# RWKV core in an fp32 model kernel: both norm sums as 512-column products, roots taken in place in PSUM

## The chip, the cores and the metric

The kernel runs on one core of one Trainium2 chip. The metric is the device time of one execution in microseconds (us); lower is better. Nothing runs on the other seven cores.

## The reference, cut to what matters

The model is a stack of blocks over 1024 tokens and 1024 channels, batch 1, all in fp32: a Hawk layer, an RWKV-7 layer, each with a SwiGLU and a gated embedding step, then a second kind of block. The change is in the RWKV-7 layer alone, in its core, which works on 16 heads of 64 channels:

```python
kk = heads(k * k_k)
kk = kk / jnp.maximum(jnp.sqrt(jnp.sum(kk * kk, axis=-1, keepdims=True)), 1e-12)
...
y = rwkv7_scan(rh, heads(decay), kh, vh, -kk, kk * ah)
mean = jnp.mean(y, axis=-1, keepdims=True)
var = jnp.mean(jnp.square(y - mean), axis=-1, keepdims=True)
yn = ((y - mean) * lax.rsqrt(var + RW_GN_EPS)).reshape(B, T, D)
yn = yn * ln_w.astype(f32) + ln_b.astype(f32)
bonus = jnp.sum(rh * kh * r_k.astype(f32), axis=-1, keepdims=True) * vh
out = (yn + bonus.reshape(B, T, D)).astype(x.dtype) * g
```

So there are two norms over the 64 channels of a head, for each token: the length of the key `kk`, and the deviation of the output `y`. Both want a sum of squares and a reciprocal root.

## The kernel before, in words

Data lie with channels on the 128 partitions and the 1024 tokens along the rows. `rw_core` takes 128 channels at a time, which is one pair of heads, so its loop over `m` has 8 passes (KD = 8), written out without a hardware loop. Tokens are worked in 16 chunks of 64 (NC = 16), two to a tile of 128 (NT = 8). In a pass:

- **grams and transposes** (L1317, L1337, L1339, L1327): products of keys and receivers within each chunk, and four transposed tensors for each tile.
- **the doubling chain**: a triangular 64x64 block of each chunk and head is inverted in five levels, each for two heads h = 0, 1. A level is `corrections` on TensorE (L1359), `keep_correction` on ScalarE (L1539 and L1541, PSUM to SBUF), `inverses` on TensorE (L1368) and `grow` on VectorE (L1718 and L1720). GpSimd masks the off-diagonal part (L1247). The last level has smaller products (L1375, L1382), and `whole` on VectorE (L1725) puts the result together.
- **solutions** (L1391), then **outputs** (L1414 and L1400), which wait for copies on ScalarE (L1588).
- **the prior pass's recurrence**: 15 small steps (`step` L1271/L1273 on TensorE, `state` L1678/L1679 on VectorE) for pair m-1 are threaded through the pass of pair m up to the second level. So the group norm of pair m-1 is taken in pass m, and the key norm of pair m+1 too.

Both norms go the same way. `token_sums` (L1279) makes 8 products whose weights are the 128x128 squares of one tile of tokens and whose moving operand is two columns of a constant (`head_mean`, 1/64 within a head); that leaves one number for each token and head, 128x16 in PSUM. `moment` on VectorE (L1623, L1626) copies the numbers to a small tile, scales them and adds or bounds; `inverse_roots` on ScalarE takes Ln and Exp of 128x32 numbers for both norms at once (L1526, L1527), each with its own table load. `spread` on TensorE (L1287) then makes 16 products with 128 columns for each norm, which bring the rates back to all 128 rows and 1024 tokens in two PSUM banks. `unit_key` (L1631) and `group_norm` (L1685) on VectorE multiply by them. A third sum, `bonus_sum`, already uses `head_sum`: two products of 512 columns with `head_mean` as data for all rows (L1263). In fp32 each of these products is two records in the trace, so `head_sum` shows as x4, `token_sums` as x16, `spread` as x32.

The order on each engine is written by hand, one queue for each engine, and semaphores join them. Around the change TensorE's queue is: `inverses` of level 1, `corrections` of level 2, `variance(m-1)`, `key_sum(m+1)`, `inverses` 2, `corrections` 3, `key_spread(m+1)`, `inverses` 3, `last_corrections`, `deviation_spread(m-1)`, `last_inverses`, `solutions`, `bonus_sum(m+1)`, `outputs`. On VectorE `group_norm(m-1)` and `key_rate(m+1)` stand ahead of `whole`. PSUM banks 2 and 3 (SUM_BANK) hold the key rates, banks 4 and 5 (STEP_BANK) the steps and later the deviation rates.

## Time and profile before

| | us |
|---|---|
| median of 3 runs | 4240.67 (4226.02 to 4241.39) |
| the profiled execution, its own time | 4249.0 |
| its span | 4247.1 |
| TensorE busy in the span | 3794.7 (89%) |
| VectorE, ScalarE, GpSimd busy | 1644.6, 981.1, 1322.8 |
| pace of the core's passes (start of L1414 in two passes) | 75.2, 75.0, 75.2, 71.7, 75.2, 71.4, and 61.0 for the last |

The profile is one execution. Engines are PE (TensorE matmul), PEld (its weight loads), DVE (VectorE), ACT (ScalarE), POOL (GpSimd). A timeline row gives start, length, engine, line, operation, output<-inputs, count, and in brackets how long the engine was idle before it and who released it. PEclk is the granted clock of TensorE: 1.00 is 2.4 GHz, 0.50 is 1.2 GHz. The core is only some 620 us of the span, from about 1863 to 2485 us.

### The profile page before, as it was taken

To read this page: it belongs to the slowest core of one execution; us is meant where nothing else is said; L and a number is where in the kernel's file an instruction comes from. 1 tells how busy PE (TensorE), PEld (TensorE's weight loads), DVE (VectorE), ACT (ScalarE), POOL (GpSimd) and SP (SyncE) were. 2 spreads that over 40 slices of the span, in tenths; PEclk is the share of its full clock that TensorE was granted. 3 is DMA by queue.
4 is the path that set the end of the run, shared out by engine and by line. 5 is a ranking of instruction groups with operands and counts; after the bars stand their busy time and mean duration, and the time that the engine had idled before them with its cause. 6 is when DMAs were issued, how large, how long until landed. Compare 5 with 4: busy or idle time off the path is not lost. (4 is left out here: it accounts for less than half of the span.)

```text
span 4247.1 us, 62128 instructions
## 1 busy us (share of the span) xinstructions
PE 3794.7 (89%) x26524; PEld 3058.4 (72%) x26524; DVE 1644.6 (39%) x1835; ACT 981.1 (23%) x1222; POOL 1322.8 (31%) x989
## 2 busy tenths in 40 slices
PE   5997999999998679978898979999999989977888
PEld 4775788888876467768787857888888777763567
DVE  5554331221344621134645533312213454157542
ACT  3552110000021632223343312100000230141221
POOL 1442233333332122222333312333333323274242
PEclk9998999999999789987878889999999999978899
DMA  2111111111110222220211021111111112100211
GB/s 80 44 41 38 35 49 45 48 46 46 43 56 29 109 81 85 82 99 27 72 37 67 18 80 40 49 45 48 46 45 44 56 38 79 50 7 1 75 45 64
DMA packets 59363, 221.80 MB, mean 52 GB/s; under 512 B 6576, under 2 KB 6832, under 8 KB 58672
## 3 DMA queue, kind: packets, MB, share of 16 engines
q1 hardware_dynamic: 49968, 185.57, 12.8%
q10 hardware_dynamic: 9216, 33.56, 2.0%
q8 instruction: 146, 2.39, 0.2%
q14 instruction: 33, 0.27, 0.0%
HBM read 181.36 MB, written 37.75 MB: 52 GB/s over the span
## 5 line engine op out<-in xcount | busy, mean ns | idle before, releaser
L141 PE MATMUL ps<-xh,whi 128*128 128x512 f32 x4160 | 1343.3, 405 | 190.3 <-DVE xl L343 48.3
L141 PE MATMUL ps<-xl,whi 128*128 128x512 f32 x4160 | 1328.9, 401 | 0.0
L141 PE MATMUL ps<-xh,wlo 128*128 128x512 f32 x4160 | 1327.9, 401 | 0.0
L141 PEld LDWEIGHTS ps<-xh,whi 128*128 128x128 f32 x4160 | 794.3, 192 | 408.3 <-issue 136.1
L141 PEld LDWEIGHTS ps<-xl,whi 128*128 128x128 f32 x4160 | 797.0, 192 | 194.9
L141 PEld LDWEIGHTS ps<-xh,wlo 128*128 128x128 f32 x4160 | 795.5, 191 | 194.3
L115 POOL TENSOR_TENSOR gap<-ones 128x1 f32<-128x1 f32 x258 | 68.6, 266 | 2352.1 <-PE ps L141 2271.8
L118 POOL TENSOR_TENSOR wlo<-wraw,whi 128x1024 fp32r<-128x1024 f32 (+3 forms) x258 | 642.9, 2492 | 21.5
L116 POOL TENSOR_SCALAR whi<-wraw 128x1024 fp32r<-128x1024 f32 (+3 forms) x258 | 285.5, 1107 | 0.0
L572 DVE TENSOR_TENSOR h<-ps,h 128x1024 f32 x56 | 68.5, 1224 | 423.9 <-PE ps L141 423.9
L644 ACT ACTIVATE sq<-sq 128x1024 f32<-128x1024 f32 x44 | 46.6, 1059 | 775.6 <-DVE sq L658 775.6
L658 DVE TENSOR_TENSOR sq<-ps,sq 128x1024 f32<-128x1024 f32 x44 | 53.9, 1225 | 319.2 <-PE ps L141 319.2
L664 DVE TENSOR_TENSOR sum_of_squares<-ps,sq 128x1024 f32<-128x1024 f32 x44 | 53.9, 1225 | 273.5 <-PE ps L141 273.1
L646 ACT ACTIVATE xh<-sum_of_squares 128x1024 f32 x44 | 46.7, 1062 | 437.5 <-DVE sum_of_squares L664 437.5
L899 DVE SCALAR_TENSOR_TENSOR mix<-rw_xn,rw_rest,mix 128x1024 f32<-128x1024 f32 x48 | 62.3, 1308 | 206.2 <-ACT mix L872 206.2
L1247 POOL TENSOR_TENSOR rw_levels<-rw_levels,rw_masks 128x512 f32<-128x512 f32 x64 | 87.4, 1378 | 171.6 <-PE ps L1359 128.4
L660 DVE TENSOR_TENSOR sq<-sq 128x1024 f32<-128x1024 f32 x44 | 103.2, 2345 | 49.5 <-ACT sq L644 49.5
L666 DVE TENSOR_TENSOR xl<-sum_of_squares,xh 128x1024 f32 x44 | 93.3, 2121 | 58.9 <-ACT xh L646 58.9
L336 DVE TENSOR_TENSOR sum_of_squares<-sum_of_squares,sq 128x1024 f32<-128x1024 f32 x48 | 86.8, 1809 | 62.5 <-ACT sq L325 41.7
L316 ACT ACTIVATE gap<-ones 128x1 f32<-128x1 f32 x56 | 11.4, 203 | 350.9 <-DVE h L572 196.2
L1368 PE MATMUL ps<-rw_inverse 64*64 64x32 f32 x2048 | 85.2, 244 | 3.6 <-ACT rw_inverse L1541 3.6
L1368 PEld LDWEIGHTS ps<-rw_inverse 64*64 64x64 f32 x2048 | 81.1, 166 | 6.3 <-ACT rw_inverse L1541 4.3
(402 smaller groups left out, 3837.3 us busy)
## 6 DMA issues: line engine op xcount, KB each, us to landing
wraw<-w_ffn_in SPq DMA_DIRECT2D x88, 512.0 KB, 3.2
rw_kept<-rw_stage ACTq DMA_DIRECT2D x48, 512.0 KB, 2.6
rw_next<-rw_kept SPq DMA_DIRECT2D x40, 512.0 KB, 5.7
wraw<-w_ffn_out SPq DMA_DIRECT2D x32, 512.0 KB, 3.2
wraw<-w_ple SPq DMA_DIRECT2D x16, 640.0 KB, 3.9
wraw<-w_b_in SPq DMA_DIRECT2D x18, 512.0 KB, 3.2
wraw<-w_hawk_in SPq DMA_DIRECT2D x10, 640.0 KB, 3.8
wraw<-w_ffn_out SPq DMA_DIRECT2D x16, 384.0 KB, 2.9
```

What stands on the lines that cost most here:

```text
L115: nc.gpsimd.tensor_tensor(g.gap[:, 0:1], g.ones[:, 0:1], g.ones[:, 0:1], ALU.mult)
L116: nc.gpsimd.tensor_scalar(g.whi[:, s, 0:w], g.wraw[:, s, 0:w], 1.0, 0.0, ALU.mult, ALU.add).then_inc(g.w_hi.sem, 1)
L118: nc.gpsimd.tensor_tensor(g.wlo[:, s, 0:w], g.wraw[:, s, 0:w], g.whi[:, s, 0:w].bitcast(F32), ALU.subtract).then_inc(g.w_split.sem, 1)
L141: last = nc.tensor.matmul(acc[:, hf, :], w[:, s, c:c + P], x[:, kt, hf * HALF:(hf + 1) * HALF], start=start and kt == 0 and n == 0, stop=s ...
L336: nc.vector.tensor_tensor(g.sumsq[:], g.sumsq[:], sq[:, s, :], ALU.add).then_inc(g.sq_used.sem, 1)
L572: nc.vector.tensor_tensor(ht, flat(banks(g, acc + 2 * s)), ht, ALU.add).then_inc(g.acc_free.sem, 1)
L658: nc.vector.tensor_tensor(sg, flat(banks(g, 0)), tmp.rstd, ALU.mult).then_inc(g.gate_scaled.sem, 1)
L660: nc.vector.tensor_tensor(sg, sg, tmp.rstd, ALU.mult).then_inc(g.up_scale.sem, 1)
L666: nc.vector.tensor_tensor(flat(hl[:, bass.ds(m, 1), :]), hid[:], flat(hh[:, bass.ds(m, 1), :]).bitcast(F32), ALU.subtract).then_inc(g.acc_ ...
L899: nc.vector.scalar_tensor_tensor(mix[:, kt % 3, :], xn[:, kt, 1:1 + T], rest[:, 8 * n + kt:8 * n + kt + 1], mix[:, kt % 3, :], ALU.mult, A ...
L1247: nc.gpsimd.tensor_tensor(halved(Nm[:, h]), twice(Nc[:, h]), mask_wide(f"off{b}"), ALU.mult).then_inc(g.off_ready.sem, 1)
L1368: last = nc.tensor.matmul(block_bank(D_BANK + h)[rows, j, :], X[rows, h, j, :], D[rows, h, j, :], start=True, stop=True)
```

## The change

Both sums become `head_sum`: 2 products of 512 columns whose result stands in all 128 rows at once, in the banks where the rates are wanted. ScalarE takes Ln and Exp over 128x1024 in place in those PSUM banks. `token_sums`, `spread` and `moment` go, with the small tiles. The lower bound of the key norm becomes a bias of 1e-37 in the Ln and a minimum of 1e12 in `unit_key`. Lines on each engine move as below.

```diff
@@ TensorE
                 def variance(m):
                     pe.wait_ge(g.dev_ready.sem, g.dev_ready.base + m + 1)
-                    token_sums(dev, DEV_AT, g.var_done)
+                    head_sum(dev, STEP_BANK, g.var_done)

                 def key_sum(m):
                     pe.wait_ge(g.kksq_ready.sem, g.kksq_ready.base + m + 1)
-                    token_sums(t1, KEY_AT, g.kksum_done)
-                def key_spread(m):
-                    pe.wait_ge(g.rates_ready.sem, g.rates_ready.base + m + 1)
-                    spread(SUM_BANK, KEY_AT, g.kkinv_ready)
-                def deviation_spread(m):
-                    pe.wait_ge(g.rates_ready.sem, g.rates_ready.base + m + 3)
-                    spread(STEP_BANK, DEV_AT, g.gn_ready)
+                    head_sum(t1, SUM_BANK, g.kksum_done)
...
                     for h in (0, 1):
                         inverses(m, 1, h)
+                    if following:
+                        pe.wait_ge(g.w_ready.sem, g.w_ready.base + 2 * m + 2)
+                        key_sum(m + 1)
                     for h in (0, 1):
                         corrections(m, 2, h)
                     if prior:
                         variance(m - 1)
-                    if following:
-                        key_sum(m + 1)
...
-                        key_spread(m + 1)
...
-                        deviation_spread(m - 1)
@@ ScalarE
-                def inverse_roots(n):
-                    act.wait_ge(g.moments_ready.sem, g.moments_ready.base + n + 1)
-                    ca.link(act, nc.scalar.activation(moments, moments, ACT.Ln))
-                    nc.scalar.activation(rates, moments, ACT.Exp, scale=-0.5).then_inc(g.rates_ready.sem, 1)
+                key_rates, deviation_rates = (g.ps[:, b:b + 2, :] for b in (SUM_BANK, STEP_BANK))
+                def log_key(m):
+                    act.wait_ge(g.kksum_done.sem, g.kksum_done.base + m + 1)
+                    nc.scalar.activation(key_rates, key_rates, ACT.Ln, scale=float(HD), bias=tiny).then_inc(g.kklog_ready.sem, 1)
+                def inverse_key(m):
+                    act.wait_ge(g.kklog_ready.sem, g.kklog_ready.base + m + 1)
+                    nc.scalar.activation(key_rates, key_rates, ACT.Exp, scale=-0.5).then_inc(g.kkinv_ready.sem, 1)
+                def log_variance(m):
+                    act.wait_ge(g.var_done.sem, g.var_done.base + m + 1)
+                    nc.scalar.activation(deviation_rates, deviation_rates, ACT.Ln, bias=norm_eps).then_inc(g.log_ready.sem, 1)
+                def inverse_deviation(m):
+                    act.wait_ge(g.log_ready.sem, g.log_ready.base + m + 1)
+                    nc.scalar.activation(deviation_rates, deviation_rates, ACT.Exp, scale=-0.5).then_inc(g.gn_ready.sem, 1)
...
                     keep_correction(m, 1, 1)
+                    if following:
+                        growth(m + 1)
                     if prior:
                         squares(m - 1)
                     keep_correction(m, 2, 0)
                     if following:
-                        growth(m + 1)
+                        log_key(m + 1)
                     keep_correction(m, 2, 1)
-                    inverse_roots(m + 1)
+                    if prior:
+                        log_variance(m - 1)
                     keep_correction(m, 3, 0)
                     if following:
-                        blend(m + 1)
+                        inverse_key(m + 1)
                     keep_correction(m, 3, 1)
                     if following:
+                        blend(m + 1)
+                    keep_correction(m, LAST, 0)
+                    if following:
                         decay_until(m + 1)
-                    keep_correction(m, LAST, 0)
                     keep_correction(m, LAST, 1)
+                    if prior:
+                        inverse_deviation(m - 1)
@@ VectorE
-                    nc.vector.tensor_tensor(halves(kk), halves(kk), g.ps[:, SUM_BANK:SUM_BANK + 2, :], ALU.mult).then_inc(g.unit_ready.sem, 1)
+                    nc.vector.scalar_tensor_tensor(halves(kk), g.ps[:, SUM_BANK:SUM_BANK + 2, :], 1e12, halves(kk), ALU.min, ALU.mult).then_inc(g.unit_ready.sem, 1)
...
-                    moment(m + 1 if following else None, m - 1 if prior else None)
                     grow(m, 2, 0)
                     grow(m, 2, 1)
                     grow(m, 3, 0)
                     if following:
                         unit_key(m + 1)
                     grow(m, 3, 1)
-                    if prior:
-                        group_norm(m - 1)
                     if following:
                         key_rate(m + 1)
                     whole(m, 0)
                     whole(m, 1)
+                    if prior:
+                        group_norm(m - 1)
```

The first and the last pass have the same edits for what they hold of it: `key_sum(0)`, `log_key(0)` and `inverse_key(0)` ahead of the loop, `variance(7)`, `log_variance(7)` and `inverse_deviation(7)` behind it.

**TensorE, from the second level to `last_inverses`**, in a pass with a prior and a following pair. Before (L1368 is `inverses`, L1359 `corrections`, L1279 the two sums, L1287 the two spreads, L1375 and L1382 the last level):

```order
L1359 MATMUL ps<-rw_inverse,rw_levels 64x32 x32
L1279 MATMUL ps<-rw_masks,rw_end 128x2 x8
L1279 MATMUL ps<-rw_masks,rw_next 128x2 x8
L1368 MATMUL ps<-rw_inverse 64x32 x32
L1359 MATMUL ps<-rw_inverse,rw_levels 64x32 x32
L1287 MATMUL ps<-ident,wraw 64x128 x16
L1368 MATMUL ps<-rw_inverse 64x32 x32
L1375 MATMUL ps<-rw_inverse,rw_levels 32x32 x32
L1287 MATMUL ps<-ident,wraw 64x128 x16
L1382 MATMUL ps<-rw_inverse 32x32 x32
L1391 MATMUL ps<-rw_tok,rw_inverse 64x128 x32
```

And now (L1344 `inverses`, L1335 `corrections`, L1261 both sums, L1351 and L1358 the last level, L1367 `solutions`):

```order
L1344 MATMUL ps<-rw_inverse 64x32 x32
L1261 MATMUL ps<-rw_next,rw_masks 128x512 x2
L1335 MATMUL ps<-rw_inverse,rw_levels 64x32 x32
L1261 MATMUL ps<-rw_end,rw_masks 128x512 x2
L1344 MATMUL ps<-rw_inverse 64x32 x32
L1335 MATMUL ps<-rw_inverse,rw_levels 64x32 x32
L1344 MATMUL ps<-rw_inverse 64x32 x32
L1351 MATMUL ps<-rw_inverse,rw_levels 32x32 x32
L1358 MATMUL ps<-rw_inverse 32x32 x32
L1367 MATMUL ps<-rw_tok,rw_inverse 64x128 x32
```

The key sum now stands ahead of the second `corrections`, both spreads are gone, and nothing but the chain itself stands between the variance sum and `solutions`.

**ScalarE, from the second level to the copies behind `solutions`.** Before (L1539 and L1541 are `keep_correction`, L1513 `growth`, L1518 `blend`, L1522 `decay_until`):

```order
L1513 ACTIVATE rw_next<-rw_next 128x1024
L1539 ACTIVATE rw_inverse<-ps,rw_masks 128x8x32 [waits x_done]
L1541 ACTIVATE rw_inverse<-ps,rw_masks 128x8x32
L1526 ACT_TABLE_LOAD
L1526 ACTIVATE wraw<-wraw 128x32 [waits moments_ready]
L1527 ACT_TABLE_LOAD
L1527 ACTIVATE wraw<-wraw 128x32 [waits act_chain]
L1539 ACTIVATE rw_inverse<-ps,rw_masks 128x8x32 [waits x_done]
L1541 ACTIVATE rw_inverse<-ps,rw_masks 128x8x32
L1518 ACTIVATE rw_next<-rw_next,rw_small,vectors 128x1024 [waits cum_ready,risen]
```

And now (L1522 and L1524 `keep_correction`, L1498 and L1502 the key's Ln and Exp, L1506 the Ln of the variance):

```order
L1498 ACT_TABLE_LOAD
L1498 ACTIVATE ps<-ps,wraw 128x1024 [waits kksum_done]
L1522 ACTIVATE rw_inverse<-ps,rw_masks 128x8x32 [waits x_done]
L1524 ACTIVATE rw_inverse<-ps,rw_masks 128x8x32
L1506 ACTIVATE ps<-ps,wraw 128x1024 [waits var_done]
L1522 ACTIVATE rw_inverse<-ps,rw_masks 128x8x32 [waits x_done]
L1524 ACTIVATE rw_inverse<-ps,rw_masks 128x8x32
L1502 ACT_TABLE_LOAD
L1502 ACTIVATE ps<-ps 128x1024 [waits kklog_ready]
L1522 ACTIVATE rw_inverse<-ps,rw_masks 128x8x32 [waits x_done]
L1524 ACTIVATE rw_inverse<-ps,rw_masks 128x8x32
L1488 ACTIVATE rw_next<-rw_next,rw_small,vectors 128x1024 [waits cum_ready,risen]
```

Each table load with its activation of 1024 columns now stands between the two halves of a level of the chain; there are two loads to a pass as before.

**VectorE, the end of the chain.** Before (L1685 is `group_norm`, L1636 `key_rate`, L1725 `whole`):

```order
L1720 STREAM_TRANSPOSE rw_inverse<-rw_inverse 128x256 [waits d_ready]
L1685 SCALAR_TENSOR_TENSOR rw_end<-rw_end,vectors,ps 128x1024 [waits gn_ready]
L1636 TENSOR_TENSOR rw_next<-rw_next 128x1024 [waits blend_ready]
L1725 SCALAR_TENSOR_TENSOR rw_inverse<-ps,rw_masks,rw_inverse 128x8x32 [waits blocks_ready,d_done] x2
L1642 SCALAR_TENSOR_TENSOR rw_next<-rw_next,vectors 128x1024 [waits rv_loaded,key_ready]
```

And now (L1668 `group_norm`, L1619 `key_rate`, L1708 `whole`):

```order
L1703 STREAM_TRANSPOSE rw_inverse<-rw_inverse 128x256 [waits d_ready]
L1619 TENSOR_TENSOR rw_next<-rw_next 128x1024 [waits blend_ready]
L1708 SCALAR_TENSOR_TENSOR rw_inverse<-ps,rw_masks,rw_inverse 128x8x32 [waits blocks_ready,d_done] x2
L1668 SCALAR_TENSOR_TENSOR rw_end<-rw_end,vectors,ps 128x1024 [waits gn_ready]
L1625 SCALAR_TENSOR_TENSOR rw_next<-rw_next,vectors 128x1024 [waits rv_loaded,key_ready]
```

`whole`, for which `solutions` waits, no longer stands behind the group norm of the prior pair.

## Rows read from the trace of the kernel before

**Rows 1.** Windows: whole core, then three stretches of pass 4 (length, busy by engine, PEclk)

```profile
1862.60:2485.30 622.70, 532.59 (x12288) 488.53 (x12288) 324.38 (x616) 233.99 (x368) 178.86 (x119) 0.81 0.13 46
2192.00:2205.00 13.00, 12.14 (x401) 11.74 (x396) 9.41 (x25) 8.40 (x14) 5.52 (x4) 1.00 0.02 4
2206.00:2222.50 16.50, 16.50 (x196) 16.36 (x195) 1.99 (x6) 8.17 (x14) 3.75 (x3) 0.50 0.01 2
2233.00:2236.50 3.50, 2.78 (x26) 2.81 (x28) 3.47 (x5) 0.00 (x0) 0.00 (x0) 0.52 0.03 7
```

**Rows 2.** Timeline of TensorE in pass 4, second level to the bonus sum

```profile
2204.17 1.10 PE L1359 MATMUL ps<-rw_inverse,rw_levels 64*64 64x32 f32 x32
2205.43 1.60 PE L1359 MATMUL ps<-rw_inverse,rw_levels 64*64 64x32 f32 x32 [0.17 <-DVE rw_inverse L1720]
2206.96 3.57 PE L1279 MATMUL ps<-rw_masks,rw_end 128*128 128x2 f32 x16
2210.40 3.55 PE L1279 MATMUL ps<-rw_masks,rw_next 128*128 128x2 f32 x16
2213.88 3.63 PE L1368 MATMUL ps<-rw_inverse 64*64 64x32 f32 x64
...
2220.85 2.96 PE L1287 MATMUL ps<-ident,wraw 128*64 128x128 f32 x32
2223.74 2.06 PE L1368 MATMUL ps<-rw_inverse 64*64 64x32 f32 x64
...
2228.41 1.97 PE L1287 MATMUL ps<-ident,wraw 128*64 128x128 f32 x32
...
2233.72 5.08 PE L1391 MATMUL ps<-rw_tok,rw_inverse 64*64 64x128 f32 x64 [2.22 <-issue]
2238.74 1.98 PE L1263 MATMUL ps<-rw_next,rw_masks 128*128 128x512 f32 x4
```

**Rows 3.** Timeline of ScalarE in pass 4

```profile
2205.32 0.47 ACT L1539 ACTIVATE rw_inverse<-ps,rw_masks 128x256 f32<-128x256 f32 x1 [1.21 <-PE ps L1359]
2205.69 0.47 ACT L1541 ACTIVATE rw_inverse<-ps,rw_masks 128x256 f32<-128x256 f32 x1
2206.05 1.05 ACT L1513 ACTIVATE rw_next<-rw_next 128x1024 f32<-128x1024 f32 x1
...
2207.93 1.28 ACT L1526 ACT_TABLE_LOAD   x1
2214.28 0.23 ACT L1526 ACTIVATE wraw<-wraw 128x32 f32<-128x32 f32 x1 [5.07 <-DVE wraw L1626]
2214.52 1.28 ACT L1527 ACT_TABLE_LOAD   x1
2215.82 0.23 ACT L1527 ACTIVATE wraw<-wraw 128x32 f32<-128x32 f32 x1
...
2237.10 1.02 ACT L1588 ACTIVATE rw_levels<-ps 128x1024 f32<-128x1024 f32 x1 [8.10 <-PE ps L1391]
```

**Rows 4.** Timeline of VectorE in pass 4

```profile
2204.38 0.42 DVE L1718 TENSOR_TENSOR rw_inverse<-ps,rw_inverse 128x256 f32<-128x256 f32 x1 [0.70 <-PE ps L1368]
2204.84 0.45 DVE L1720 STREAM_TRANSPOSE rw_inverse<-rw_inverse 128x256 f32<-128x256 f32 x1
2213.99 0.17 DVE L1623 TENSOR_SCALAR wraw<-ps 128x16 f32<-128x16 f32 x1 [8.70 <-PE ps L1279]
...
2230.42 1.28 DVE L1685 SCALAR_TENSOR_TENSOR rw_end<-rw_end,vectors,ps 128x1024 f32<-128x1024 f32 x1 [2.69 <-PE ps L1287]
...
2232.75 0.87 DVE L1725 SCALAR_TENSOR_TENSOR rw_inverse<-ps,rw_masks,rw_inverse 128x256 f32<-128x256 f32 x2
```

**Rows 5.** Timeline: TensorE's `solutions` of passes 0 and 7, the last variance sum

```profile
1936.58 5.17 PE L1391 MATMUL ps<-rw_tok,rw_inverse 64*64 64x128 f32 x64 [0.86 <-DVE rw_inverse L1725]
...
2443.39 3.71 PE L1391 MATMUL ps<-rw_tok,rw_inverse 64*64 64x128 f32 x64 [0.98 <-issue]
...
2473.45 3.57 PE L1279 MATMUL ps<-rw_masks,rw_end 128*128 128x2 f32 x16 [1.42 <-ACT rw_end L1531]
```

More of the change, by code:

```diff
@@ L1128, in rw_core @@
         k_rest, pc = small[:, 0:KD], small[:, KD:KD + NC]
-        moments, rates = (g.wraw[:, 0, KD * P + 2 * HD + n * 4 * NT:KD * P + 2 * HD + (n + 1) * 4 * NT] for n in (0, 1))
-        KEY_AT, DEV_AT = 0, 2 * NT
+        tiny, norm_eps = (g.wraw[:, 0, KD * P + 2 * HD + n:KD * P + 2 * HD + n + 1] for n in (0, 1))
         sw, a, r, kx, v, c, e1, e2, kk, t1 = (nxt[:, n, :] for n in range(10))
@@ L1163, in rw_core @@
         halves = lambda ap: ap.rearrange("p (a b) -> p a b", a=2)
-        sums = g.ps[:, STEP_BANK, 0:P]
         step_bank = lambda cc: g.ps[:, STEP_BANK + cc % 2, 0:2 * CH]
@@ L1274, in step @@
                     last.then_inc(g.st_done.sem, 1)
-                def token_sums(src, at, done):
-                    for j in range(NT):
-                        last = nc.tensor.matmul(sums[:, at + 2 * j:at + 2 * j + 2], src[:, j * P:(j + 1) * P], head_mean[:, 0:P:HD], start=True, stop=True)
-                    last.then_inc(done.sem, 1)
-                def spread(b, at, done):
-                    for j in range(NT):
-                        for h, hd in enumerate(heads):
-                            rate = rates[:, at + 2 * j + h:at + 2 * j + h + 1].broadcast_to([P, HD])
-                            last = nc.tensor.matmul(g.ps[hd, b + j // 4, j % 4 * P:(j % 4 + 1) * P], rate, g.ident[:], start=True, stop=True)
-                    last.then_inc(done.sem, 1)
                 def variance(m):
                     pe.wait_ge(g.dev_ready.sem, g.dev_ready.base + m + 1)
-                    token_sums(dev, DEV_AT, g.var_done)
+                    head_sum(dev, STEP_BANK, g.var_done)
                 def key_sum(m):
                     pe.wait_ge(g.kksq_ready.sem, g.kksq_ready.base + m + 1)
-                    token_sums(t1, KEY_AT, g.kksum_done)
-                def key_spread(m):
-                    pe.wait_ge(g.rates_ready.sem, g.rates_ready.base + m + 1)
-                    spread(SUM_BANK, KEY_AT, g.kkinv_ready)
-                def deviation_spread(m):
-                    pe.wait_ge(g.rates_ready.sem, g.rates_ready.base + m + 3)
-                    spread(STEP_BANK, DEV_AT, g.gn_ready)
+                    head_sum(t1, SUM_BANK, g.kksum_done)
                 def bonus_sum(m):
@@ L1546, in _ @@
                 key_square(0)
-                inverse_roots(0)
+                log_key(0)
+                inverse_key(0)
                 decay(0)
@@ L1595, in _ @@
                 squares(KD - 1)
-                inverse_roots(KD + 1)
+                log_variance(KD - 1)
+                inverse_deviation(KD - 1)
             @block.vector
@@ L1618, in decay_before @@
                         ins.then_inc(g.cum_ready.sem, 1)
-                def moment(key, dev_of):
-                    if key is not None:
-                        dve.wait_ge(g.kksum_done.sem, g.kksum_done.base + key + 1)
-                        ins = nc.vector.tensor_scalar(moments[:, KEY_AT:KEY_AT + 2 * NT], sums[:, KEY_AT:KEY_AT + 2 * NT], float(HD), 1e-24, ALU.mult, ALU.max)
-                    if dev_of is not None:
-                        dve.wait_ge(g.var_done.sem, g.var_done.base + dev_of + 1)
-                        ins = nc.vector.tensor_scalar(moments[:, DEV_AT:DEV_AT + 2 * NT], sums[:, DEV_AT:DEV_AT + 2 * NT], 1.0, GN_EPS, ALU.mult, ALU.add)
-                    ins.then_inc(g.moments_ready.sem, 1)
                 def unit_key(m):
                     dve.wait_ge(g.kkinv_ready.sem, g.kkinv_ready.base + m + 1)
-                    nc.vector.tensor_tensor(halves(kk), halves(kk), g.ps[:, SUM_BANK:SUM_BANK + 2, :], ALU.mult).then_inc(g.unit_ready.sem, 1)
+                    nc.vector.scalar_tensor_tensor(halves(kk), g.ps[:, SUM_BANK:SUM_BANK + 2, :], 1e12, halves(kk), ALU.min, ALU.mult).then_inc(g.unit_ready.sem, 1)
                 def key_rate(m):
@@ L1735, in _ @@
                 decay_before(0, 1)
-                moment(0, None)
                 unit_key(0)
@@ L1829, in _ @@
                     state(KD - 1, cc)
-                moment(None, KD - 1)
                 group_norm(KD - 1)
@@ L1844 @@
                 ("mask_loaded", 16), ("rw_loaded", 48 * KD), ("rv_loaded", 32 * KD), ("gate_loaded", 16 * KD), ("att_stored", 16 * KD),
-                ("rest_ready", 1), ("moments_ready", KD + 2), ("rates_ready", KD + 2)])
+                ("rest_ready", 1)])
 NH = 8
@@ L2828, in make_signals @@
     g.gram_ar = signal("gram_ar")
-    g.moments_ready = signal("moments_ready")
+    g.kklog_ready = signal("kklog_ready")
     g.out_hm = signal("out_hm")
-    g.rates_ready = signal("rates_ready")
+    g.log_ready = signal("log_ready")
     g.rest_ready = signal("rest_ready")
```

10 lines of the change are left out of this document (3 added, 7 removed).

## The prediction

> **What bounds the kernel now.** I read the windows first. The core is 622.7 us of a span of 4247, with a mean granted clock of 0.81 [rows 1]; all that changes is in it. It has 8 passes, and the paces in the table (75.2 to 71.4 us) say that they repeat, so I follow pass 4 by its timelines. The reader is to see three things. First, from 2206.96 to 2233.72 TensorE hardly rests: sums, chain and spreads stand in one queue, and the chain is late because the norms stand in it [rows 2]. Second, this happens at half clock: from 2206 to 2222.5 TensorE is busy 16.50 of 16.50 us at 0.50, that is 1.2 GHz, while the 13 us before it ran at 1.00 [rows 1]; 64 records of `inverses` take 3.63 us there and 2.06 us after the clock has risen [rows 2]. Third, `solutions` start at 2233.72, right behind `whole` (two from 2232.75, done at 2233.62), and `whole` stood behind `group_norm` at 2230.42, which had waited for the second spread [rows 2, 4]. The bracket says "issue", but the end of `whole` fits to 0.1 us. So the time of a pass from the second level to `solutions` is TensorE's queue, then VectorE's behind a spread.
>
> **The change, step by step, in pass 4.** The point of comparison is the start of `solutions`, 2233.72. I walk the new queues from 2204.17, where the second `corrections` began. Prices, all from rows: a half level of 32 records on TensorE 1.0 at high clock (2.06 for two), 1.8 at low (3.63 for two); `head_sum` 1.98, 1.9 to the next start [rows 2]; `keep_correction` 0.84 (two of 0.47, 0.37 apart) [rows 3]; `grow` 0.91 (2204.38 to 2205.29) [rows 4]; a table load 1.28 [rows 3].
>
> The Ln and Exp of 1024 columns in place in PSUM are not in this trace. Nearest are a PSUM to SBUF copy of the same shape, 1.02, and an Exp from SBUF to SBUF, 1.05; the one of 32 columns takes 0.23 [rows 3]. No row writes PSUM from ScalarE, so the ends are 0.85 (the copy less its overlap with a neighbour, some 0.1 to 0.2) and 2.1 (twice the copy). I take 1.05, by the row of the same function.
>
> - *Removed on TensorE:* two sums, 2206.96 to 2213.88, and two spreads, 2220.85 to 2223.74 and 1.9 at 2228.41 [rows 2]: 11.7 us. *Added:* two `head_sum`, 3.8. `moment` (0.17 [rows 4]) goes; `unit_key` stays one pass over PSUM, at most the 1.28 of `group_norm`, which is of its kind [rows 4]; it lies in the wait for level 3 and would cost 0.1 without that cover.
> - *Key sum* at 2204.2, as `key_square` and the w copies are done by then; `corrections` 2 from 2206.1 to 2208.1; variance to 2210.0. `squares` is 1.05 later behind `growth`, ready near 2205.3, so it is covered.
> - *ScalarE, level 2:* keep at 2207.2, done 2208.1; load and Ln (1.28 + 1.05) to 2210.4; the other keep to 2211.3. `inverses` 2 run 2210.0 to 2212.3: only 0.3 is lost. `log_variance` fits behind, to 2212.3. In a queue this is the new wait: behind Ln stands the second keep, and for it the second half of TensorE's level.
> - *Level 3:* `corrections` 2212.3 to 2214.3. Keep to 2214.2; load and Exp to 2216.6; second keep to 2217.4. The second `inverses` cannot start before 2217.5, though TensorE is free at 2215.3: 2.2 us of new idle time.
> - *Last level:* at high clock `inverses` 1.0, `grow` 0.9, last corrections 0.7, keep behind `decay_until`, last inverses 0.6, `whole` 0.5, gives 2222.4. At low clock from about 2214 it gives 2224.0 (`inverses` 1.8, the two small products 1.0 each). I take 2224.0: the stretch from 2210 on has only 32-column products and gaps, as the stretches had before the clock fell.
> - *Behind it:* `group_norm` needs `inverse_deviation`, ready about 2223.4, and is no longer ahead of `whole`. `solutions` are as slow as before (5.08 [rows 2], begun at low clock then too: 0.52 in 2233 to 2236.5 [rows 1]), so their cost does not change. The next thing to be late would be GpSimd's `hats`, behind `group_bias` and `gated`; by the same walk they end within 1 us of when TensorE wants them, so I count nothing.
>
> Gain of a full pass: 2233.7 - 2224.0 = 9.7 us. The six passes 1 to 6 give 58. Pass 0 has only the key norm: the same walk from its second level ends near 1930.8 against 1936.58 [rows 5], 5.8. Pass 7 has only the variance: one spread and one sum at mixed clock less 1.9, and the lower levels in part at high clock, 7 before 2443.39 [rows 5]. Ahead of the loop the key norm ends some 2 us sooner, but `blend`, behind it on ScalarE, is not sooner: 0. At the end the variance of pair 7 is alone: before, 3.57 for the sum [rows 5], 0.2, then 0.23 + 1.28 + 0.23 [rows 3], then a spread; now a sum at low clock (twice 1.9), Ln 1.05, load and Exp 2.33: 2 less. Sum 58 + 5.8 + 7 + 2 = 73. The profiled execution took 4249.0, so it would take 4176; the median is 8.3 lower than that execution, so 4168.
>
> The Trainium skill's page "ScalarE: Activation LUTs", section "What ACT_TABLE_LOAD costs", speaks against this place for the loads: it gives 1.28 us for the load and 1.38 more for a drain with each switch. By it both half levels would wait 1.4 us longer, 2.8 in each of 7 passes, some 19 in all, and the time would be 4187. The trace has a load of 1.28 between an activation that ends at 2214.51 and one that starts at 2215.82 [rows 3]: no drain is seen, so I leave it out of the sum.
>
> **Rivals.**
>
> *B, the clock stays as it is now.* The fall at 2206 comes before the first removed product, amid the chain's 32-column products [rows 1, 2]. If the two sums of 512 columns don't hold it up, everything from 2206 to 2223 runs at 1.2 GHz: `corrections` 2 to 2209.6, variance (3.7) to 2213.1, three half-clock pairs to 2223.5, with 0.7 for Exp, `solutions` at 2228.7; as the clock rose at 2223 before, some 1 us less. Gain 5 to 7 in a pass, 46 in all with 10 for the ends: 4195. For it: the fall did not wait for the 2-column sums. Against: those are 7 us of nearly no columns within the low stretch, and in their place come 3.8 us of dense ones. The Trainium skill's page "TensorE: Matmul & The Clock Gate", section "What's actually happening", says that the gate follows how busy the array has been recently. The trace disagrees if busy means busy time: 16.50 of 16.50 us at half clock. By that rule the new idle gaps would make the clock no better, which is this rival.
>
> *C, the clock stays high through the chain.* `solutions` at 2222.4 and themselves at high clock, 3.71 as in pass 7 [rows 5], against 5.08. Then `hats` bind after about 1 us. Gain 11.5 in a pass, 87 in all: 4154. For it: 13 us of 32-column products with a few wider ones ran at 1.00 [rows 1]. Against: from 2210 on nothing wide is left, and the gaps are larger.
>
> *D, ScalarE is dearer than I think*: an activation in place takes the 2.1 of the upper end, or a load waits as long for other reasons. Two of them hold a half level, so 2.1 in each of 7 passes and as much at the end, some 17 less gain: 4185. For it, that reading and writing PSUM at once is in no row; against it, the 1.02 for reading [rows 3].
>
> *E, slower.* ScalarE becomes the bound. Two activations of 1024 columns stand within the chain, and two more beside it. If one in place in PSUM cost 1.05 + x, a pass would lose 2x at once and up to 4x when ScalarE is full; the gain of 9.7 is gone at x = 2.4 to 4.9. At 4.5 us each (x = 3.45) all four count: 13.8 - 9.7 = 4.1 in a pass, some 30 in all, 4271. For it only that no row writes PSUM from ScalarE; against it, that the copy out of PSUM is no dearer than Exp in SBUF [rows 3].
>
> *F, no difference:* a later wait takes the gain, such as `hats`, or TensorE's fetch gaps at the start of a pass. It would have to be 7 us or more in each pass, and I find only 1.
>
> **How the numbers follow.** Forecast 0.50, B 0.22, C 0.12, D 0.09, F 0.04, E 0.03. The likeliest case alone reaches from 4158 to 4180. The range of 4143 to 4205 takes in B, C and D, with the 15 us over which the three runs lie (4226 to 4241), and leaves out E, F and the outer parts of the others. Over 0.5% (21 us, about what a measurement of this kernel can tell) faster are the forecast, B, C and D with some doubt: 0.91; same 0.05; slower 0.04.
>
> **What would show each step.** In the new profile the stretch from the first `head_sum` of a pass to its `solutions` should be near 20 us (it was 26.8 from the first sum, and 29.5 from the second `corrections`). `head_sum` in the chain should read 1.98 for x4, not 3.7; if 3.7, B. ScalarE's Ln and Exp should read near 1.05; 2 or more means D or E. TensorE should show an idle of about 2 us in level 3, released by `keep_correction`. The low stretch should be under 12 us for a pass, against 16.5. The pass should pace at 64 to 66 us. The prediction is wrong if the pace moves by less than 5 us while the sums read 1.98, for then another engine holds the pass.

## The result, and the profile after

The changed kernel takes 4171.27 us (median of 4 runs, 4165.62 to 4182.99), the kernel before 4240.05 in the same comparison: ratio 0.9849, 95% interval 0.9818 to 0.988. It is faster by 1.5%, 69 us. The prediction said 4168. The profiled execution took 4175.08 with a span of 4173.2, against 4249.0 and 4247.1.

Windows of the changed kernel, as [rows 1]: the core, then pass 4 from the key sum on.

```profile
1860.60:2411.40 550.80, 461.11 (x11584) 393.52 (x11584) 325.20 (x600) 261.54 (x380) 183.94 (x119) 0.85 0.14 51
2172.00:2183.00 11.00, 10.63 (x227) 7.89 (x224) 2.82 (x7) 7.48 (x12) 4.35 (x3) 1.00 0.01 1
2183.00:2196.50 13.50, 11.88 (x240) 11.31 (x238) 9.01 (x12) 7.06 (x10) 3.44 (x2) 0.50 0.01 2
```

The core went from 622.7 us to 550.8, and TensorE's busy time in it from 532.6 to 461.1. The stretch with both sums and level 2 runs at 1.00 now; the clock falls at 2183, at the end of the third `corrections`.

TensorE in pass 4, as [rows 2] (L1344 `inverses`, L1335 `corrections`, L1261 the sums, L1351 the last level, L1367 `solutions`):

```profile
2172.80 1.98 PE L1261 MATMUL ps<-rw_next,rw_masks 128*128 128x512 f32 x4
2174.72 2.06 PE L1335 MATMUL ps<-rw_inverse,rw_levels 64*64 64x32 f32 x64
2176.70 1.98 PE L1261 MATMUL ps<-rw_end,rw_masks 128*128 128x512 f32 x4
2178.61 1.12 PE L1344 MATMUL ps<-rw_inverse 64*64 64x32 f32 x32
2179.94 1.12 PE L1344 MATMUL ps<-rw_inverse 64*64 64x32 f32 x32 [0.20 <-ACT rw_inverse L1524]
2180.89 1.10 PE L1335 MATMUL ps<-rw_inverse,rw_levels 64*64 64x32 f32 x32
2182.16 1.30 PE L1335 MATMUL ps<-rw_inverse,rw_levels 64*64 64x32 f32 x32 [0.17 <-DVE rw_inverse L1703]
2183.21 1.95 PE L1344 MATMUL ps<-rw_inverse 64*64 64x32 f32 x32
2186.00 1.92 PE L1344 MATMUL ps<-rw_inverse 64*64 64x32 f32 x32 [0.84 <-ACT rw_inverse L1524]
...
2192.48 5.69 PE L1367 MATMUL ps<-rw_tok,rw_inverse 64*64 64x128 f32 x64 [0.63 <-issue]
```

From the key sum to `solutions` it is 19.68 us; the walk of the prediction had 19.8. The waits for ScalarE are where it put them: 0.20 in level 2, behind Ln, and 0.84 in level 3, behind Exp, where the walk had 2.2 at high clock.

ScalarE in pass 4, as [rows 3]:

```profile
2176.26 0.47 ACT L1524 ACTIVATE rw_inverse<-ps,rw_masks 128x256 f32<-128x256 f32 x1
2176.74 1.28 ACT L1498 ACT_TABLE_LOAD   x1
2178.04 1.09 ACT L1498 ACTIVATE ps<-ps,wraw 128x1024 f32<-128x1024 f32 x1
...
2182.41 0.47 ACT L1524 ACTIVATE rw_inverse<-ps,rw_masks 128x256 f32<-128x256 f32 x1
2182.89 1.28 ACT L1502 ACT_TABLE_LOAD   x1
2184.19 1.01 ACT L1502 ACTIVATE ps<-ps 128x1024 f32<-128x1024 f32 x1
2185.11 0.47 ACT L1522 ACTIVATE rw_inverse<-ps,rw_masks 128x256 f32<-128x256 f32 x1
...
2190.63 1.02 ACT L1510 ACTIVATE ps<-ps 128x1024 f32<-128x1024 f32 x1
```

Ln in place in PSUM takes 1.09 with a bias from memory, Exp 1.01. The load starts 0.01 us behind the end of the activation before it (2176.73, then 2182.88), and the activation behind it starts 0.02 us after its end: no drain is to be seen.

VectorE in pass 4, as [rows 4]: `whole` twice, then `group_norm` behind it.

```profile
2191.90 0.48 DVE L1708 SCALAR_TENSOR_TENSOR rw_inverse<-ps,rw_masks,rw_inverse 128x256 f32<-128x256 f32 x1 [0.71 <-PE ps L1358]
2192.30 1.27 DVE L1668 SCALAR_TENSOR_TENSOR rw_end<-rw_end,vectors,ps 128x1024 f32<-128x1024 f32 x1
```

`whole` waits for TensorE's last inverses and for nothing of the norms. The pass is shorter where the change was made: of 10.6 us, 10.4 lie between the end of `inverses` 1 and `solutions` (30.2 and 19.8 in the mean of passes 1 to 6). The next table has the means over passes 1 to 6, taken from the starts of three TensorE groups in the timelines (the receiver gram L1327, `solutions` L1391, outputs L1414, and L1303, L1367, L1390 now):

| passes 1 to 6, mean us | before | changed |
|---|---|---|
| receiver gram to `solutions` | 44.7 | 34.2 |
| `solutions` to outputs | 7.0 | 7.3 |
| outputs to the next receiver gram | 22.2 | 21.8 |
| pace of a pass | 73.9 | 63.4 |

The 73.9 us between the two profiled executions lie so: passes 1 to 6 give 63.4, pass 7 gives 7.3 (61.0 to 53.7), the end 3.1 (from the last outputs to the next stage's first product, 48.5 to 45.4), pass 0 with its prologue costs 1.8 (78.6 to 80.4, from the first key sum to the outputs), and 2.0 come from ahead of the core, which the change does not touch. (That both the pace now and the gain of the six passes are 63.4 is chance.)

### The profile page after: what moved, and what is told of

Its sections match the earlier page's. It is cut to its first block and busy times, and to the rows that moved or that the text cites. A ratio compares the mean times of both kernels' runs of the same rounds, so it can differ in the third digit from the quotient of the medians.

```text
span 4173.2 us, 60717 instructions
## 1 busy us (share of the span) xinstructions
PE 3719.1 (89%) x25820; PEld 2963.1 (71%) x25820; DVE 1647.9 (39%) x1820; ACT 1008.8 (24%) x1234; POOL 1330.2 (32%) x989
## 5 line engine op out<-in xcount | busy, mean ns | idle before, releaser
L1344 PE MATMUL ps<-rw_inverse 64*64 64x32 f32 x2048 | 78.1, 230 | 15.9 <-ACT rw_inverse L1524 15.9
L1344 PEld LDWEIGHTS ps<-rw_inverse 64*64 64x64 f32 x2048 | 72.7, 148 | 24.0 <-ACT rw_inverse L1524 18.3
```

The source lines that it names most:

```text
L1344: last = nc.tensor.matmul(block_bank(D_BANK + h)[rows, j, :], X[rows, h, j, :], D[rows, h, j, :], start=True, stop=True)
```

## The experiments

The forecast time came out, but its sum had two kinds of terms that the trace alone cannot part: queue time, and the clock. The theory at the start: TensorE's queue of sums and spreads held the chain, mostly at 1.2 GHz. The rivals: it is the place of `group_norm`; it is the clock alone. All runs compute the whole output; what is added is read by nothing. The last two columns are read from each profiled execution: the mean pace of passes 1 to 6, and the time at 1.2 GHz between the first receiver gram and the last outputs, in windows of 0.5 us.

| kernel | median us | ratio to before, 95% | pace | low clock |
|---|---|---|---|---|
| before | 4240 to 4246 | 1 | 73.9 | 191.5 |
| changed | 4171.27 | 0.9849 [0.9818, 0.988] | 63.4 | 112.5 |
| changed, again | 4175.2 | 0.9842 [0.9821, 0.9863] | 61.6 | 95.5 |
| before, norm behind whole | 4218.69 | 0.9946 [0.9928, 0.9964] | 69.5 | 143 |
| changed, norm ahead again | 4194.83 | 0.9879 [0.9858, 0.99] | 66.6 | 127 |
| before, wide products added | 4249.13 | 1.0011 [0.9998, 1.0023] | 73.8 | 177 |
| changed, spreads added back | 4182.91 | 0.9856 [0.9833, 0.9878] | 63.6 | 44.5 |
| changed, narrow sums added | 4213.77 | 0.9925 [0.9903, 0.9947] | 68.3 | 160.5 |
| changed, key sum back | 4183.94 | 0.9862 [0.9836, 0.9887] | 64.6 | 140 |
| changed, Exp behind the half | 4162.76 | 0.9809 [0.9776, 0.9841] | 62.2 | 96 |
| changed, Ln and Exp behind | 4158.2 | 0.9805 [0.977, 0.9839] | 60.9 | 76 |
| changed, wide in the gap | 4178.93 | 0.9846 [0.9812, 0.988] | 63.7 | 92.5 |
| Ln and Exp behind, one spread | 4144.88 | 0.977 [0.975, 0.9791] | 60.0 | 33.5 |
| Ln and Exp behind, two spreads | 4160.67 | 0.9803 [0.9781, 0.9825] | 62.6 | 34.5 |

The two profiled executions of the changed kernel, 4175.08 and 4163.05, differ by 12 us, 1.8 us in the pace. The pace of one execution is therefore good to 2 us, no better, and the low time of the core to some 17; the ratios carry the verdicts. The runs stand in three groups on three chips, so between groups a difference of medians is read beside that of the ratios.

### The place of the group norm

```diff
@@ VectorE, kernel before
-                    if prior:
-                        group_norm(m - 1)
                     if following:
                         key_rate(m + 1)
                     whole(m, 0)
                     whole(m, 1)
+                    if prior:
+                        group_norm(m - 1)
```

> The kernel before with one edit of the change: group_norm behind whole on VectorE, nothing else. My theory (TensorE's queue of sums and spreads holds the chain, at half clock): the second spread still stands ahead of the last inverses, so solutions start only some 1.5 us sooner in passes 1 to 7, 10 us in all: about 4230, ratio 0.997. Rival, that the place of group_norm behind the second spread is what held solutions: its wait and its 1.2 us go, 3 us or more in a pass, 4220 or less, and a good part of the 69 us.

Measured: 4218.69, 0.54% faster, 23 us (the kernel before 4243.51 beside it): twice what I expected, and what the rival had (4220 or less, and 4.4 us in the pace). But 23 us is only a third of the gain, so the place of the norm is one cause and not the whole. Its timeline in pass 4, TensorE's last level with the second spread, then `solutions`:

```profile
2205.94 1.97 PE L1287 MATMUL ps<-ident,wraw 128*64 128x128 f32 x32
2207.84 1.20 PE L1382 MATMUL ps<-rw_inverse 32*32 32x32 f32 x64
2209.67 3.71 PE L1391 MATMUL ps<-rw_tok,rw_inverse 64*64 64x128 f32 x64 [0.63 <-issue]
```

The idle time ahead of `solutions` falls from 2.22 [rows 2] to 0.63: those are the 1.6 us that I had counted. But `solutions` also take 3.71 instead of 5.08, since the clock no longer falls in the gap: before, it fell at 2233.2, within the wait, and here it is high from 2200.5 on. In passes 1 to 6 the way from `solutions` to the outputs is 5.56 each time, against 6.87 to 7.15 before. So 1.6 us less of waiting went with 3.0 us less of time.

The same edit undone in the changed kernel:

> The changed kernel with that edit undone: group_norm ahead of key_rate and whole again. ScalarE's inverse_deviation ends just when whole could start, so whole waits for it and for 1.2 us of group_norm: 1.4 us in each of 7 passes, 10 us, about 4181. If the place of group_norm is most of the gain, 4200 or more.

Measured: 4194.83, ratio 0.9879 against 0.9849 and 0.9842 without the edit, some 14 us slower where I expected 10, with intervals that overlap at their ends. VectorE of that run in pass 4, then TensorE:

```profile
2197.42 1.28 DVE L1668 SCALAR_TENSOR_TENSOR rw_end<-rw_end,vectors,ps 128x1024 f32<-128x1024 f32 x1 [2.59 <-ACT ps L1510]
2198.62 1.22 DVE L1619 TENSOR_TENSOR rw_next<-rw_next 128x1024 f32<-128x1024 f32 x1
2199.75 0.87 DVE L1708 SCALAR_TENSOR_TENSOR rw_inverse<-ps,rw_masks,rw_inverse 128x256 f32<-128x256 f32 x2
```

```profile
2200.72 5.62 PE L1367 MATMUL ps<-rw_tok,rw_inverse 64*64 64x128 f32 x64 [3.13 <-issue]
```

`whole` waits for `group_norm` and for `key_rate` behind it; I had counted the first only. TensorE idles 3.13 us ahead of `solutions`, against 0.63. Here the longer wait costs no more than its length: `solutions` take 5.62 behind 3.13 us of wait and 5.69 behind 0.63, since they start at low clock in both. From either kernel the place of the norm is worth 14 to 23 us, a fifth to a third of the gain.

### Spreads and sums, each put back as work that nothing reads

```diff
@@ TensorE, changed kernel: spreads
+                    if following:
+                        old_spread()
                     for h in (0, 1):
                         inverses(m, 3, h)
                     for h in (0, 1):
                         last_corrections(m, h)
+                    if prior:
+                        old_spread()
```

> The changed kernel plus the two old spreads (16 products of 128 columns each, on a constant, into banks that nothing reads) at their old places in TensorE's queue. Theory: the first falls partly into the idle of level 3 and costs about 1 us, the second 1.9 us, 3 us in a pass less what the clock gives back: 4171 + 15 to 25 = 4186 to 4196. Rival, the spreads were the main cost at half clock (3.7 us each): 4171 + 45 or more. Rival, wide products help the clock more than they cost: 4171 or less.

Measured: 4182.91, ratio 0.9856, which cannot be told from the changed kernel (0.9842 and 0.9849); it is less than I expected (4186 to 4196), and the intervals leave room for less than 20 us, so the rival of 45 or more falls. TensorE in pass 4 of that run, from level 3 (L1350 `inverses`, L1291 the spreads, L1373 `solutions`):

```profile
2179.32 3.24 PE L1291 MATMUL ps<-ident,wraw 128*64 128x128 f32 x32
2182.49 2.05 PE L1350 MATMUL ps<-rw_inverse 64*64 64x32 f32 x64
...
2187.16 1.97 PE L1291 MATMUL ps<-ident,wraw 128*64 128x128 f32 x32
2189.05 1.20 PE L1364 MATMUL ps<-rw_inverse 32*32 32x32 f32 x64
2190.89 3.71 PE L1373 MATMUL ps<-rw_tok,rw_inverse 64*64 64x128 f32 x64 [0.63 <-issue]
```

From start to start the two spreads take 5.1 us of queue here (3.17 and 1.89), and the pass is no longer (63.6, against 63.4 and 61.6). In the mean of passes 1 to 6, `solutions` come 2.0 us later (36.3 us behind the receiver gram, against 34.2), and the outputs follow them 1.8 us sooner (5.6, against 7.3). Behind them the half levels run at 1.0 instead of 1.9 us, the last level at 1.20, and `solutions` at 3.71 instead of 5.69. The time at 1.2 GHz in the core fell from 112.5 to 44.5 us. So in this kernel the products of 128 columns paid for themselves by the clock, and taking them out was worth little or nothing. I had counted 4.8 us of queue for them in a pass. What is put back here is their time on TensorE alone; nothing waits for them, as `group_norm` did for the second one before.

```diff
@@ TensorE, changed kernel: narrow sums (8 products of 2 columns each)
                     if prior:
                         variance(m - 1)
+                        narrow_sums(dev, 0)
+                    if following:
+                        narrow_sums(t1, 2 * NT)
```

> The changed kernel plus the old sums: 16 products of 2 columns (8 on dev, 8 on t1) at their old place behind the second corrections, written where nothing reads. The run with the old spreads added back lost almost nothing, and its low stretches all but went. New theory: the narrow sums are what the kernel before paid for, by their 7 us of queue and by the clock, which stays low while they run. Then this run loses 7 us or more in a pass with a low stretch as long as before (over 16 us in a pass): 4171 + 50 to 65 = 4221 to 4236. Rival, the narrow sums cost only their queue time at high clock, 2 us each, and hide partly in the idle of levels 2 and 3: 4171 + 15 to 30.

Measured: 4213.77, ratio 0.9925. That is 0.8% over the changed kernel, 34 us, between the two numbers. TensorE in pass 4 of that run (L1290 the narrow sums):

```profile
2186.07 1.98 PE L1261 MATMUL ps<-rw_end,rw_masks 128*128 128x512 f32 x4
2187.89 1.84 PE L1290 MATMUL ps<-rw_masks,rw_end 128*128 128x2 f32 x16
2189.60 2.88 PE L1290 MATMUL ps<-rw_masks,rw_next 128*128 128x2 f32 x16
```

Here the clock falls within the second group: 1.84 at high, 2.88 half way, where the kernel before had 3.57 and 3.55 [rows 2]. The time at low clock rises from 112.5 (95.5 in the second execution) to 160.5 us. Half of that is time, if all that runs there takes twice as long: 24 to 33 of the 34 us by this estimate. But the two groups take 4.5 us of queue in pass 4 (2187.89 to 2192.41) and would take some 3.4 at high clock throughout (twice the 1.71 of the first), so queue time and clock both have a part, and the runs do not part them. Of the single edits the narrow sums are the largest.

### Does dense work hold the clock?

> The kernel before plus work that nothing reads: 4 products of 256 columns (as many columns as one head_sum, 8 records) on TensorE between inverses 1 and corrections 2 of each pass. Theory with the clock in it: 1.9 us more queue, but the fall near the second corrections comes later, so the low stretch of 13 to 27 us in a pass shrinks; no slower than before, or up to 4 us faster in a pass (4210 to 4240). Rival, the clock takes no notice of it and the whole gain was queue time: 1.9 us more at high clock or 3.7 at low in 8 passes, 4255 to 4270.

```diff
+                def wide():
+                    for b in (X_BANK, X_BANK + 1):
+                        for n in (0, 1):
+                            nc.tensor.matmul(g.ps[:, b, HALF // 2:HALF], head_mean, head_mean_wide, start=True, stop=True)
...
                     for h in (0, 1):
                         inverses(m, 1, h)
+                    wide()
                     for h in (0, 1):
                         corrections(m, 2, h)
```

Measured: 4249.13, ratio 1.0011, interval 0.9998 to 1.0023: no difference that can be told. That agrees with the weakest of what I expected, no slower than before, and not with the 15 us and more of the rival. The low time fell by only 14.5 us, to 177. The added work (1.9 us, eight times) cost 2.7 us in pass 0 and 1.5 in pass 7, and nothing that shows in passes 1 to 6 (pace 73.8 against 73.9, each good to 2 us). So most of it was given back by the clock, but it did not hold the clock through the narrow sums and the two levels behind it. It speaks against "the clock alone": the wide products without the removal of the narrow ones gain nothing.

> The changed kernel plus 4 products of 256 columns that nothing reads, on TensorE between corrections 3 and inverses 3, where it idles for ScalarE's Exp. If dense columns hold the clock, the low stretch of some 10 to 13 us behind it shrinks to under 5 us in a pass: it gives back 3 to 4 us (solutions at 5 us instead of 5.7, half levels at 1.0 instead of 1.8) and costs about 1: 4171 - 15 = 4156. If the clock takes no notice: 4171 + 8 to 15.

The same four products, into banks 6 and 7, stood between `corrections` 3 and `inverses` 3 of the changed kernel. Measured: 4178.93, ratio 0.9846: nothing gained, nothing lost, and not the 15 us that I had for the case that wide products hold the clock. From the end of level 1 to `solutions` the low time is 6.4 us in the mean of passes 1 to 6, against 8.2 and 7.6, so it hardly fell. In pass 4 the clock had fallen ahead of the products, and they took 3.78, against 2.00 for the same four at high clock in the run before:

```profile
2180.77 1.90 PE L1342 MATMUL ps<-rw_inverse,rw_levels 64*64 64x32 f32 x32 [0.17 <-DVE rw_inverse L1711]
2182.60 3.78 PE L1292 MATMUL ps<-rw_masks 128*128 128x256 f32 x8
2186.31 2.65 PE L1351 MATMUL ps<-rw_inverse 64*64 64x32 f32 x64
```

They stand in TensorE's queue ahead of the half level that the chain waits for, so what level 3 gained by the clock behind them was paid ahead of it.

### The order on ScalarE, and a faster version

```diff
@@ ScalarE, changed kernel (in the first run only the second pair of edits, the Exp)
                     keep_correction(m, 2, 0)
-                    if following:
-                        log_key(m + 1)
                     keep_correction(m, 2, 1)
+                    if following:
+                        log_key(m + 1)
...
                     keep_correction(m, 3, 0)
-                    if following:
-                        inverse_key(m + 1)
                     keep_correction(m, 3, 1)
+                    if following:
+                        inverse_key(m + 1)
@@ VectorE
                     grow(m, 3, 0)
-                    if following:
-                        unit_key(m + 1)
                     grow(m, 3, 1)
+                    if following:
+                        unit_key(m + 1)
```

> The changed kernel with the key's Exp (and its table load) behind the second keep_correction of level 3 on ScalarE, and unit_key behind grow(3,1) on VectorE. The second inverses of level 3 no longer wait for load and Exp (0.84 us idle in pass 4, more at high clock). But unit_key and key_rate now stand ahead of whole. My walk: 1 us in each of 7 passes, 7 us: 4164. If ScalarE's order costs nothing because VectorE's queue ahead of whole takes it back: 4171. If the idle was the whole loss and the clock follows: 4155.

> As the run before, and the key's Ln behind the second keep_correction of level 2 too. The half level of level 2 waited only 0.20 us for it, so 1 us more over all passes: 4163. If Ln then pushes log_variance into level 3's first keep: 4170 or more.

Measured: 4162.76 (0.9809) and 4158.2 (0.9805), where I expected 4164 and 4163. Both are 8 to 17 us under the changed kernel's two medians, by the ratios 14 to 19; the intervals overlap, and what the Ln adds cannot be told. The direction is that of the walk: a load and an activation between two half levels hold TensorE. It is likely, not settled.

> The changed kernel itself once more, beside the next three on the same chip, since the medians of the kernel before moved by 6 us between calls. Expected ratio to before 0.983 to 0.986; what a run of the others gains is read against this one.

> The changed kernel with the key sum back behind the second corrections and the variance sum. ScalarE's Ln then waits for the second 512-column sum, and the second keep_correction of level 2 behind it comes 1.9 us later: 1.5 to 2 us in each of 7 passes, 11 to 14 us more than the changed kernel. If TensorE's queue alone counts, the same as the changed kernel.

```diff
@@ TensorE, changed kernel
-                    if following:
-                        pe.wait_ge(g.w_ready.sem, g.w_ready.base + 2 * m + 2)
-                        key_sum(m + 1)
                     for h in (0, 1):
                         corrections(m, 2, h)
                     if prior:
                         variance(m - 1)
+                    if following:
+                        pe.wait_ge(g.w_ready.sem, g.w_ready.base + 2 * m + 2)
+                        key_sum(m + 1)
```

Measured: 4183.94, ratio 0.9862 beside 0.9842 for the changed kernel on the same chip: 9 us slower by the medians, 11 to 14 expected, and the intervals overlap. The early place of the key sum may be worth this; it is not settled.

> Ln and Exp behind the second halves, plus one old spread (16 products of 128 columns that nothing reads) between last_corrections and last_inverses in each pass. With the old spreads added back the stretch from solutions to outputs took 5.6 us in a pass, without them 6.9 to 8.5, as solutions began at low clock. If the wide products ahead of solutions do this, it falls to 5.6 here, 2 us less, for 1.9 us more queue of which 0.6 is idle now: 4158 - 5 = 4153, low clock in the core under 60 us. If queue time is all: 4158 + 10.

> The same with both old spreads, the first ahead of inverses 3. There is no idle left there to hide it, so it costs 1.9 us in a pass and saves the low stretch of 2 to 6 us, half of which is time: even, 4150 to 4160. Low clock in the core 30 us or less.

```diff
@@ TensorE, kernel with Ln and Exp behind the halves (one spread)
                     for h in (0, 1):
                         last_corrections(m, h)
+                    old_spread()
                     for h in (0, 1):
                         last_inverses(m, h)
```

Measured: one spread 4144.88, ratio 0.977 with interval 0.975 to 0.9791, clear of the changed kernel's 0.9821 to 0.9863 in the same comparison: 30 us faster. Two spreads: 4160.67, 0.9803. A window of the one-spread run over a stretch of pass 4, and its TensorE from the last corrections to the outputs:

```profile
2150.00:2192.00 42.00, 37.10 (x1022) 31.17 (x1018) 26.57 (x35) 23.09 (x33) 16.82 (x12) 0.96 0.18 65
```

```profile
2165.26 1.00 PE L1357 MATMUL ps<-rw_inverse,rw_levels 32*32 32x32 f32 x32 [0.24 <-DVE rw_inverse L1710]
2166.19 3.23 PE L1291 MATMUL ps<-ident,wraw 128*64 128x128 f32 x32
2169.34 1.20 PE L1364 MATMUL ps<-rw_inverse 32*32 32x32 f32 x64
2171.18 3.71 PE L1373 MATMUL ps<-rw_tok,rw_inverse 64*64 64x128 f32 x64 [0.63 <-issue]
2174.82 1.99 PE L1261 MATMUL ps<-rw_next,rw_masks 128*128 128x512 f32 x4
2176.73 1.98 PE L1396 MATMUL ps<-rw_tok,rw_levels 64*64 64x128 f32 x64
```

The clock falls in the last corrections and has risen again before the spread ends; `solutions` take 3.71, and from their start to the outputs it is 5.55 us, as expected, against 6.9 to 8.5 in the changed kernel. The low time in the core is 33.5 us. It is the fastest version measured.

How much of it the added spread gives is less sure. Against the same order without it (4158.2, 0.9805) it is 13 us by the medians and 15 by the ratios, with intervals that overlap, though all four runs lie below all four. By the two profiled executions (4157.69 and 4144.84) `solutions` come no later (32.8 us behind the receiver gram, against 32.7) and the outputs follow 2.2 us sooner (5.6, against 7.8), but the way from there to the next receiver gram is 1.2 longer, so the pace goes from 60.9 to 60.0. From the first sum to the next stage's first product it is 6.7 us less (541.7 to 535.0). Another 7.2 lie behind the core (1751.2 to 1744.0), in instructions that are the same in both; the low time there is 167 us, against 185. Against the changed kernel beside it (4163.05) that stretch has 4.1 us of the 18.2 between the two profiled executions. Whether the fall of the clock there follows from the edit, no run shows.

The second spread finds no idle time to lie in and costs more than it gives; I expected 4150 to 4160.

## Why the prediction was right, point by point

**What bounded the kernel** was read rightly in its place: nearly all the gain lies from the second level to `solutions` (10.4 of 10.6 us of a pass), and GpSimd's hats took none of it (22.2 us from the outputs to the next receiver gram before, 21.8 now).

**The walk of pass 4** held to 0.1 us: 19.68 against 19.8. It held on the way too: from the key sum it had the second half of level 3 at 13.3 and the fall of the clock at 9.8, and they came at 13.2 and 10.1. The price of 1.05 for Ln and Exp in place was right (1.09 and 1.01), so rivals D and E fell. The table load costs 1.28 between two activations; by the drain of 1.38 us that the Trainium skill's page "ScalarE: Activation LUTs" adds (section "What ACT_TABLE_LOAD costs") the time would, as an estimate, have been 4187. The trace disagrees: the load and the activations around it stand 0.01 and 0.02 us apart. The waits came where they were put, 0.20 and 0.84 us; the second was less than 2.2 mostly because the first half of `inverses` 3 ran at low clock (1.95 instead of 1.0) and filled it.

**The clock** came near the forecast, with passes on both sides of it: the `head_sum` in passes 1 to 6 took 1.98 as forecast, save the key sums of passes 2 and 3 (3.68 and 3.66), and the low stretch of pass 4 was 13.5 us against 16.5, where I had said under 12. From the end of `inverses` 1 to `solutions` the low time was 9.5 us in pass 4, where the walk had 10, and from 4.0 to 11.1 in passes 1 to 6; it was 13.8 to 27.8 before. In the second profiled execution all of them took 1.98. B fell for these passes. `solutions` were not as slow as before but slower, 5.69 against 5.08. Passes differ: from 33.0 to 35.7 us between receiver gram and `solutions`. So the gain of passes 1 to 6 was 63.4 us and not the 58 that pass 4 gave, and the pace 63.4, below the 64 to 66 that I had named.

**The step that failed is pass 0.** I had 5.8 us less for it; with its prologue it took 1.8 more (the prologue 0.3 less, the pass 2.1 more). The walk was carried over from pass 4 with its clock, and here the clock was another. TensorE of the changed kernel in pass 0, the key sum and `solutions`:

```profile
1911.57 3.78 PE L1261 MATMUL ps<-rw_next,rw_masks 128*128 128x512 f32 x4
...
1935.20 6.32 PE L1367 MATMUL ps<-rw_tok,rw_inverse 64*64 64x128 f32 x64 [0.59 <-DVE rw_inverse L1708]
```

The clock fell ahead of the key sum and again behind level 2, and the pass ran much as rival B describes. In the second profiled execution of the same kernel pass 0 took 2.7 us less, which is still only 0.6 less than before: where the fall lands differs between executions of one kernel. Part of the close total is therefore luck. Of the 73.9 us between the profiled executions pass 0 gave 7.6 less than its term; passes 1 to 6 gave 5.4 more, the end 1.1 more, and 2.0 came from ahead of the core, for which no term stood.

**Terms were mis-sized and made up for each other.** The spreads were in the sum as 4.8 us of queue in a pass, and putting them back costs at most a part of that, since they paid by the clock. The narrow sums were in it as 6.9 us, some 48 in seven passes, and putting them back costs about 34. Against these two, which were too large, the place of `group_norm` was worth 14 to 23 us where I had counted 10, and the added products may cost less than their queue: as many columns as one `head_sum` has, added to the kernel before, cost 5 us (1 less to 10 more, by the interval) and not the 15 of eight times 1.9. The total of the single edits (34 for the narrow sums, 14 to 23 for the norm's place, about 9 for the key sum, 0 to 5 for the spreads) is 57 to 71, and 69 was measured. This is no proof that nothing is missing: the two added `head_sum` and the two waits for ScalarE, which cost time, are not in it, the term of the key sum is not settled, and edits that act through the clock need not add up. The share of clock and of queue in each is argued from the low times, not measured apart.

## What to carry to other kernels

Read the granted clock beside the time of a product on TensorE, and test a removal by putting the work back. Here, in a chain of small products, two groups of eight weights with two columns cost some 34 us and went with 48 us more at 1.2 GHz, while two groups of 128 columns cost nothing that can be told and went with 68 us less. A wait that another engine imposes just ahead of a large group costs its length, and more if the clock falls in it (1.6 us of wait went with 3.0 us in the kernel before; in the changed kernel, whose clock was low there anyway, it was the length alone). So move norms and side work behind the operation that the chain waits for. On ScalarE, try to keep a table load with a long activation out from between the two halves of a level (likely 14 to 19 us here).

## What the runs showed that I had not expected

Work that computes nothing can cost nothing, and perhaps give: 16 products of 128 columns for each pass, put ahead of the last inverses, go with 30 us less than the changed kernel, together with the new order on ScalarE, which alone gave 8 to 17. Half of what the products add to that lies behind the core, so some 7 us are what the core shows for them. Busy time as the profile has it does not decide the clock here: TensorE was busy for 16.50 of 16.50 us at 1.2 GHz in the kernel before [rows 1], and in the changed kernel with two groups of 128 columns added the core was at 1.2 GHz for 44.5 us instead of 112.5. The Trainium skill's page "TensorE: Matmul & The Clock Gate" (section "What's actually happening") lets the gate follow how busy the array has been; read as busy time, the trace disagrees. And the same kernel differs by up to 17 us between its executions (4165.62 to 4182.99); the two that were profiled have their falls of clock at other places.
